# Blocks of 32 in the triangular inverse from the second token block on, and split weights kept in DRAM

## What is computed

```python
lower = jnp.where(strict, beta[..., :, None] * kk * decay, 0.0)      # 64 x 64 per chunk and head
a_mat = eye + lower
sol = lax.linalg.triangular_solve(a_mat, rhs, left_side=True, lower=True, unit_diagonal=True)

h = modulate(rmsnorm(x, norm_mix_w), shift_a, scale_a); proj = h @ w_in
x = x + gate_a * (mixed @ w_out)
h = modulate(rmsnorm(x, norm_mlp_w), shift_m, scale_m)
x = x + gate_m * (jnp.square(jax.nn.relu(h @ w_ff1)) @ w_ff2)
```

## Time and profile before

| | us |
|---|---|
| median of 3 runs | 2733.97 (2733.09 to 2736.82) |
| the profiled execution, own time | 2730.9 |
| its span, first to last instruction | 2729.1 |
| PE busy / DVE / ACT / POOL in the span | 2664.8 / 1455.1 / 1057.0 / 1619.6 |
| DMA moved in the span | 311.49 MB, 34% of the 16 engines' time |

### The profile page before, as it was taken

How to read it: one execution, slowest core, us unless ns; L and a number is a source line. 1 busy time by engine, 2 the same in 40 slices (tenths; PEclk the granted TensorE clock), 3 DMA queues, 4 the chain that set the end, 5 groups by cost and what they waited for, 6 DMA issues and landing times.

```text
span 2729.1 us, 36096 instructions
## 1 busy us (share of the span) xinstructions
PE 2664.8 (98%) x13088; PEld 2214.6 (81%) x13088; DVE 1455.1 (53%) x2935; ACT 1057.0 (39%) x1831; POOL 1619.6 (59%) x1244
## 2 busy tenths in 40 slices
PE   5999999999999999999999999999999999999998
PEld 4788888888887878888887888888888888888886
DVE  5877776555567465645456445663535453322223
ACT  3533333353434333533345324353333333443332
POOL 3755555475666655665556656575555566765653
PEclk9999999999999999999999999999999999999999
DMA  7333454333343234222332323422222224232232
GB/s 281 113 133 128 158 184 156 125 114 105 97 153 102 97 97 143 89 93 83 107 117 96 105 78 116 143 85 89 89 89 85 90 85 143 93 101 93 95 130 85
DMA packets 98240, 311.49 MB, mean 114 GB/s; under 512 B 11536, under 2 KB 11664, under 8 KB 95888
## 3 DMA queue, kind: packets, MB, share of 16 engines
q1 hardware_dynamic: 67248, 246.79, 27.1%
q10 hardware_dynamic: 30816, 62.40, 7.0%
HBM read 285.03 MB, written 24.12 MB: 113 GB/s over the span
## 4 chain that ended last, share of the span: by engine, by line
PE 85%; DVE 8%; issue 3%; DMA 1%; ACT 1%; POOL 1%; ACTq 0%; SPq 0%; DVEq 0%; POOLq 0%
PE acc L516 25%; PE acc L518 25%; PE acc L517 24%; PE pm L551 5%; PE pm L556 1%; DVE mixing L1251 1%; DMA mixing<-in_ada_w 1%; DVE x L1543 1%; PE pm L655 1%; PE pm L606 1%; PE pm L650 1%; PE pm L665 1%; DVE mixing L1293 1%; PE pm L666 0%; PE pm L651 0%
## 5 line engine op out<-in xcount | busy, mean ns | idle before, releaser
L1711 POOL TENSOR_TENSOR w<-raw,w 128x512 fp32r<-128x512 f32 x832 | 1113.0, 1340 | 927.3 <-ACT w L762 924.7
L762 ACT ACTIVATE w<-raw 128x512 fp32r<-128x512 f32 x832 | 522.1, 628 | 752.2 <-PE acc L518 677.8
L516 PE MATMUL acc<-mT,w 128*128 128x512 f32 x1536 | 621.5, 405 | 7.3 <-DVE mT L1605 3.3
L518 PE MATMUL acc<-mT,w 128*128 128x512 f32 x1536 | 601.2, 391 | 0.0
L517 PE MATMUL acc<-mT,w 128*128 128x512 f32 x1536 | 599.9, 391 | 0.0
L516 PE MATMUL acc<-hid,w 128*128 128x512 f32 x864 | 348.1, 403 | 2.2 <-DVE ffs L1503 1.4
L516 PEld LDWEIGHTS acc<-mT,w 128*128 128x128 f32 x1536 | 290.1, 189 | 66.9 <-issue 5.0
L518 PEld LDWEIGHTS acc<-mT,w 128*128 128x128 f32 x1536 | 289.1, 188 | 62.7
L518 PE MATMUL acc<-hid,w 128*128 128x512 f32 x864 | 337.4, 391 | 0.0
L517 PE MATMUL acc<-hid,w 128*128 128x512 f32 x864 | 336.7, 390 | 0.0
L517 PEld LDWEIGHTS acc<-mT,w 128*128 128x128 f32 x1536 | 290.4, 189 | 54.8 <-issue 1.0
(11 more groups left out here) (239 smaller groups left out, 3558.3 us busy)
## 6 DMA issues: line engine op xcount, KB each, us to landing
raw<-in_w_all SPq DMA_DIRECT2D x416, 512.0 KB, 3.5
ada_late<-in_ada_w SPq DMA_DIRECT2D x32, 512.0 KB, 5.4
xr<-in_xT ACTq DMA_DIRECT2D x48, 256.0 KB, 4.0
mixing<-in_ada_w SPq DMA_DIRECT2D x8, 1024.0 KB, 9.9
proj_kept<-ffs ACTq DMA_DIRECT2D x32, 256.0 KB, 2.2
out<-io ACTq DMA_DIRECT2D x32, 256.0 KB, 2.5
mixed_kept<-mixing ACTq DMA_DIRECT2D x28, 256.0 KB, 2.0
xr<-mixed_kept ACTq DMA_DIRECT2D x28, 256.0 KB, 2.8
```

The lines of the kernel that those rows point to most:

```text
L516: e.matmul(bank, whi, x[:, 0, :], start=first, stop=False)
L518: m = e.matmul(bank, wlo, x[:, 0, :], start=False, stop=last)
L762: e.activation(w2[:, 0, local % HALVES, :], raw[:, tile % NRAW, local % 2 * NT:(local % 2 + 1) * NT], ACT.Copy).then_inc(S["w_hi"], 1)
L1711: e.tensor_tensor(w2[:, 1, local % HALVES, :], raw[:, tile % NRAW, local % 2 * NT:(local % 2 + 1) * NT], w2[:, 0, local % HALVES, :].bitca ...
```

## The change

1. **Blocks of 32.** Units 0 to 3 stay as they are. From unit 4 on (`wide(n)`) DVE inverts blocks of 32: 31 steps instead of 15, on 128 columns instead of 64, two to a slot in slots 20 to 35, with 2 row buffers instead of 4. `U` and `T` follow at slot 35 instead of 29. PE does the product with the level mask at slot 36 instead of 32 and `four(bB, X, U)` at slot 38 instead of 34; the two products with `Q`, of slots 36 and 38, and the two subtractions L1382 are gone, and L1387 subtracts `bB`. ACT's copy to X moves from slot 32 to 36. The small tiles move from `octs` into `swp`.
2. **Kept weights.** From window 4 on, a tile that is met for the first time is split as before, and SP also stores both parts of it (1 MB, as two halves) to a DRAM tensor `w_kept`. All later meetings, 256 tiles, are loaded from there straight into `w2`, 512 KB for each half, without ACT or POOL. 160 tiles are split, 104 of them stored.
3. **Around it.** Semaphores are merged or added (`gate_pe`, `ut_first`, `slot0` to `slot3`); three more mask tiles and a second small identity are made at the start; the wait for `attn_ready` moves from slot 38 to 46 on PE.

The core of the diff:

```diff
+SPLIT_RANK, KEPT_BY = {}, {}
+for _g, _tile in enumerate(TILES):
+    _w = weight_index(_tile)
+    if _w not in KEPT_BY:
+        SPLIT_RANK[_g] = len(SPLIT_RANK)
+        if 8 * _g >= WINDOWS[HEADS][0]:
+            KEPT_BY[_w] = _g
...
+                    maker = KEPT_BY[weight_index(TILES[g])]
+                    for half in range(2):
+                        local, made = 2 * g + half, 2 * maker + half
+                        e.wait_ge(SLOTSEM[made % HALVES], slot_count(made) + 16)
+                        e.wait_ge(S["w_used"], local - HALVES + 1)
+                        if (local - HALVES) // 2 in STORED:
+                            e.wait_ge(SLOTSEM[local % HALVES], slot_count(local))
+                        e.dma_start(w2[:, :, local % HALVES, :].bitcast(F32), w_kept[STORED[maker], half]).then_inc(
+                            SLOTSEM[local % HALVES], 16)
+
+            def store(g):
+                for half in range(2):
+                    local = 2 * g + half
+                    e.wait_ge(S["w_lo"], 2 * SPLIT_RANK[g] + half + 1)
+                    e.dma_start(w_kept[STORED[g], half], w2[:, :, local % HALVES, :].bitcast(F32)).then_inc(SLOTSEM[local % HALVES], 16)
...
             for g in range(NRAW, len(TILES)):
+                if g - 2 in STORED:
+                    store(g - 2)
                 load(g)
...
-                if s == 32:
+                if s == (36 if wide(n) else 32):
...
-                if s == 34:
+                if s == (38 if wide(n) else 34):
...
-                if s == 36:
+                if s == 36 and not wide(n):
                     e.wait_ge(S["q_ready"], 2 * n + 1)
                     four(bB, X, Q).then_inc(S["y_out"], 1)
-                if s == 38:
+                if s == 38 and not wide(n):
...
                 for i in (2 * (s - 20), 2 * (s - 20) + 1):
-                    if not (20 <= s < 28 and i < OCT - 1):
+                    if not 0 <= i < block_of(n) - 1:
                         continue
...
-                if s == 29:
-                    e.wait_ge(S["oct_steps"], OSTEPS * (n + 1))
+                if s == (35 if wide(n) else 29):
+                    whole = [P, SUB, P // block_of(n), block_of(n)]
+                    e.wait_ge(S["oct_steps"], steps_done(n + 1))
```

More of the change, by code:

```diff
@@ L34, with wide, block_of, rows_of @@
 HALVES = 4
[L35 to L38, removed]
+WIDE_FROM = HEADS
+def wide(n):
+    return n >= WIDE_FROM
+def block_of(n):
+    return 32 if wide(n) else 16
+def rows_of(n):
+    return 2 if wide(n) else 4
+def block_steps(n):
+    return 1 + 3 * (block_of(n) - 1)
+def steps_done(n):
+    return sum(block_steps(q) for q in range(n))
+def y_done(n):
+    return sum(2 if wide(q) else 4 for q in range(n))
 SLOTS = 64
@@ L154, in weight_index, with slot_count @@
     return HEADS * UNIT + KT + 2 * FFG * x + (FFG if kind == FF2 else 0) + y
+SPLIT_RANK, KEPT_BY = {}, {}
[5 more added lines that the diff above has]
+            KEPT_BY[_w] = _g
+STORED = {_g: _i for _i, _g in enumerate(KEPT_BY.values())}
+def slot_count(local):
+    return 16 * sum(at // 2 in STORED or at // 2 not in SPLIT_RANK for at in range(local % HALVES, local, HALVES))
 HIDDEN_AFTER = {}
@@ L1345, in mix @@
                     e.tensor_tensor(LT, bB, bD, ALU.mult).then_inc(S["lt_ready"], 1)
+                inverse, part = inverse_of(n), in_blocks(n, block_tile(n, 1))
                 if s == 19:
                     e.wait_ge(S["oct_masked"], n + 1)
-                    e.tensor_reduce(near, by_oct(Lm).rearrange("p t b j -> p t j b"), AX.X, ALU.add).then_inc(S["oct_steps"], 1)
-                    e.wait_ge(S["oct_steps"], OSTEPS * n + 1)
-                    for i in range(ROWS):
+                    e.wait_ge(S["r_upd"], n + 1)
+                    e.tensor_reduce(in_blocks(n, block_tile(n, 0)), by_block(n, Lm).rearrange("p t b j -> p t j b"), AX.X,
+                                    ALU.add).then_inc(S["oct_steps"], 1)
+                    e.wait_ge(S["oct_steps"], steps_done(n) + 1)
+                    for i in range(rows_of(n)):
@@ L1375, in mix @@
+                if s in (34, 36) and not wide(n):
                     at = (s - 34) // 2
-                    e.wait_ge(S["y_out"], YSTEPS * n + at + 1)
-                    e.wait_ge(S["u_first"], n + 1)
+                    e.wait_ge(S["y_out"], y_done(n) + at + 1)
+                    e.wait_ge(S["ut_first"], 2 * n + 1)
                     if at == 0:
@@ L1851, in constants @@
     masks[:, 3] = r[:, None] > r[None, :]
-    same = r[:, None] // OCT == r[None, :] // OCT
-    masks[:, 4] = -1.0 * (same & (r[:, None] < r[None, :]))
-    masks[:, 5] = same
-    for l in range(4, 6):
-        m = 1 << l
-        masks[:, 6] += ((r[:, None] // (2 * m) == r[None, :] // (2 * m))
-                           & (r[:, None] // m % 2 == 0) & (r[None, :] // m % 2 == 1))
+    for at, block in ((4, 16), (7, 32)):
+        same = r[:, None] // block == r[None, :] // block
+        masks[:, at] = -1.0 * (same & (r[:, None] < r[None, :]))
+        masks[:, at + 1] = same
+        masks[:, at + 2] = (r[:, None] // 64 == r[None, :] // 64) & (r[:, None] // block < r[None, :] // block)
     inv = (10000.0 ** (-np.arange(0, DK, 2, dtype=f) / f(DK))).astype(f)
```

148 lines of the change are left out of this document (86 added, 62 removed).

## The result

The changed kernel takes 2774.1 us (median of 4 runs, 2773.0 to 2776.2) against 2733.9 in the same comparison: ratio 1.0147, 95% interval 1.0135 to 1.0159. It is slower, as forecast, and inside the stated range, but 31 us above the forecast figure. Its profiled execution took 2774.8 us.

What follows compares the result with a forecast made beforehand. PE's instruction stream was taken to set the end. 2730.9 - 21.4 (blocks) + 28.5 (overruns) + 9 (queue) - 7 (relief) = 2740.0 us, with the median 3.1 higher: 2743, range 2713 to 2788.

Steps and rivals of the forecast that it cites:

- case A: Slots 20 to 36: DVE becomes the bound, PE waits for T and acc beyond the blocks removed; 2730 to 2765, chance 0.52.
- rival D: DVE's three instructions per step run strictly one after the other, 0.87 us a step; 2788 us, chance 0.10.
- removed blocks: PE, units 4 to 15: two products with Q go per unit, 12 x 2 x 0.89 us, -21.4 us.
- the step: DVE, one inversion step on 128 columns takes 0.73 us from multiply to multiply, instead of 0.53.
- Rival B: Slots 20 to 36: overruns stay below 21.4 us, so the kernel gets faster, 2713 to 2723 us; chance 0.28.
- DVE's overrun: Slots 20 to 36: PE waits for DVE's excess work, 28.5 us over the units, plus 9 for early idle time.
- the queue's early idle: DVE around slot 35: a full queue loses its early idle time, 1.3 us in each of seven units, +9.
- a sign of B: DVE idle time inside the stretches of units 5, 6 and 15 would show the faster rival, chance 0.28.
- The relief, -7: POOL's dropped work shortens DVE instructions reading twice from SBUF, about 1 us in seven full units from 8 on.
- DMA, 0: Stores and kept loads cost PE nothing, covered by about 5 us of lead; bounds 0 and +64 us.
- rival C: Units 4 to 9 become DMA bound, stores and loads slowing each other, +64 us, 2807; chance 0.10.

Runs made afterwards that it cites:

- experiment 2: The changed kernel with only the blocks of 32 from unit 4 on, every tile split as before (also called kernel 2): 2769.7 us, ratio 1.0130.
- experiment 1: The changed kernel with only the kept weights, blocks of 16 in all units: 2739.9 us, ratio 1.0020.
- experiment 10: The changed kernel with blocks of 32 only in units 4 and 7 to 14, PE's steps two slots later, DVE's steps last in each slot, kept weights: 2722.3 us.
- experiment 6: The changed kernel with 16 to 48 unread matmuls on PE in slot 36 of six units and 16 at slot 31 of units 4, 8, 12: 2760.0 us.
- kernel 7: The changed kernel with the product with T and the three PE steps after it two slots later in the wide units: 2752.9 us, ratio 1.0076.

## Why the prediction was right, and where its terms were off

**Direction, place and step.** The mechanism of case A came true: DVE is the bound in slots 20 to 36, and PE stands for its products. Its size did not: 2774 lies above A's own range of 2730 to 2765. The stated range held only because it ran on to 2788 for rival D, whose mechanism did not happen. That part of the hit is luck. The removed blocks (192 matmuls) and the step (0.73 us) are as forecast. Rival B fell: it needed a step below 0.69 or twice the relief. D fell with the starts of the shuffle.

**DVE's overrun, +37.6 before the relief.** This sum held, in part because its errors offset each other. Forecast by unit (overrun, and 1.3 for the queue's early idle) against PE's waits of over 0.4 us in slots 20 to 36, from PE's order of time:

| unit | 4 | 5 | 6 | 7 | 8 | 9 | 10 | 11 | 12 | 13 | 14 | 15 | sum |
|---|---|---|---|---|---|---|---|---|---|---|---|---|---|
| forecast | 1.7 | 6.3 | 9.2 | 0 | 3.1 | 1.3 | 3.4 | 0 | 3.1 | 1.3 | 1.3 | 6.9 | 37.6 |
| waits | 1.95 | 6.60 | 6.47 | 0 | 2.80 | 1.95 | 3.81 | 1.55 | 1.95 | 1.98 | 1.96 | 5.83 | 36.9 |

The size agrees, the place only in part: in units 5, 6 and 15 PE waits 18.9 us and not 22.4, in the others 18.0 and not 15.2. The prediction named two places where PE stops, T and the evacuations. In units 4, 8 and 12 it is a third, the column sums at slot 31 (1.95, 2.80, 1.95 us), in unit 11 a fourth, the gate copy at slot 34. All four are consumers of the one queue that holds the steps. DVE also kept 1.4 to 2.2 us of idle time in the stretches of units 5, 6 and 15, which the prediction had named as a sign of B; it did not save PE the waits.

**The relief, -7.** It did not come in the stretches; experiment 2 puts it at 0.7 us there. The step that failed is reading one L1406 of 1.68 us as the usual case, where the mean of 0.77 stood beside it. POOL's relief of DVE, 61 us of busy time, fell where PE seldom waits for DVE.

**DMA, 0.** Right for what was argued: no wait names a kept tile at DMA shares of 0.81 to 0.86 in the stretches of units 4 to 6, so rival C fell. The forecast 0.87 was for the whole of unit 6, which came out at 0.75 (262 GB/s where 277 were forecast). The bandwidth was not the risk, the order was: in unit 9 a raw load behind kept ones is late, and it falls on ACT. Alone the kept weights cost 5.8 us (experiment 1), beside later steps nothing that shows (experiment 10). The prediction had named that queue ("behind a raw load that is late wait ACT's `hi` and all evacuations") and priced it at 0.

**The missing term, about +24.** Every wait was priced at its length alone. Of the eleven units with a wait in the table, the clock falls to the lower level at ten, all but unit 11, and the matmuls behind are slower; filling the waits with unread work gave 14 us back (experiment 6), and the clock's records of the two traces give all 24. The term that the prediction left out is this one: it had no price for PE's clock at all, and so took a wait of 2 us for 2 us and not for nearly 4. The time itself follows the clock between executions of one kernel: kernel 7 took 2748.5 at a mean clock of 0.992 and 2760.1 at 0.987, and 0.005 x 2760 = 14 us is what that difference costs in lost work at most.

**The ledger of the two profiled spans:** -21.4 (blocks), +35.8 (waits in the stretches, 36.9 less 1.1 that PE stood idle there before), +5.6 (the rest of PE's added idle time of 41.4: units 1 to 3, and 8, 9 and 12 outside the stretches, less what units 10 and 16 gained), +24 (clock), sum +44.0 against +43.9 measured. The 24 is the difference of busy times and takes the removed blocks at 0.89 us each; the records of the clock give 24.4 without that price. Forecast was +9.1 (-21.4, +37.5, -7). The 35 us between are 24 for the clock, 7 for the relief and 5.6 for the waits outside, less 1.7 by which the stretches came out below the forecast.

## What to carry to other kernels

Price a wait of the engine that sets the end by its length and by what the clock costs behind it: here the second was two thirds of the first, 24 to 37 us. Room in a stretch is not enough. List every consumer of the busy queue in that stretch, with its place, because the first that stands behind the new work stops the critical engine. A long chain that is needed only at its end goes last in each slot of an in-order queue, its consumer as late as the schedule allows, and only in the units whose stretch has room; with that the same change, in nine of its twelve units, went from 1.5% slower to 0.4% faster. Relief of a shared port is worth something only where the critical engine waits for the relieved one.

## What the runs showed of the hardware

PE's clock can fall after a wait as short as 2 us, and does not always. Kernel 2 has the same wait of 1.98 us for T in unit 13 as the changed kernel, and there the clock stayed at 1.00; in the 5.6 us from the start of the wait PE started 23 matmuls instead of 13:

```profile
1975.20:1980.80 5.60, 3.62 (x23) 3.19 (x23) 3.02 (x6) 1.92 (x4) 1.35 (x2) 1.00 0.12 47
```

In kernel 2 the clock falls at only five of the same eleven units. The time lost per wait thus differs between kernels with equal waits, and a comparison of two such kernels carries some us of it: kernel 2 and the changed kernel both have 105.7 us of idle time, and their mean clocks are 0.989 and 0.985. What decides whether it falls is not shown.

It also falls without any wait. In the kernel before, PE does 32 matmuls of 2 columns in a row and counts as busy for 3.92 us; the stretch behind them, from 475.6 us, is at the lower level:

```profile
472.40 3.92 PE L680 MATMUL pm<-consts,x 128*128 128x2 f32 x32
475.60:479.00 3.40, 3.40 (x11) 2.82 (x12) 1.44 (x4) 0.00 (x0) 1.89 (x2) 0.50 0.75 259
```

The same comes after the 32 such matmuls at 433.34 us. So PE's busy share doesn't show every place where the clock is lost.

A 512 KB raw load takes 4.8 to 5.5 us to land (median by unit) in units 4 to 7, where the DMA engines carry 249 to 274 GB/s, and 3.5 us in the same units of the kernel before, at 124 GB/s in unit 6; no wait of PE names it. And the shared ports between DVE and POOL are lost by whoever comes second: the delay of 1.1 us goes to DVE or to POOL by a shift of 0.7 us in their starts.
